# Inverting attention denominators four key steps later in the heads of two groups

## The reference

```python
def trunk_block(x, mods, g1, g2, w1, w2, mixer):
    sh1, sc1, gt1, sh2, sc2, gt2 = mods
    mixed, ctx_tensors = mixer(modulate(rmsnorm(x, g1), sh1, sc1))
    x = x + gt1 * mixed
    hh = modulate(rmsnorm(x, g2), sh2, sc2)
    x = x + gt2 * (jnp.square(jax.nn.relu(hh @ w1)) @ w2)
    return x, ctx_tensors
...
def swa_latent(q, k, v, kc, vc, sink):
    ...
    p = jax.nn.softmax(jnp.concatenate([s_loc, s_ctx, s_sink], axis=-1), axis=-1)
    ...
    out = (jnp.einsum('bnhgqk,bnkhd->bnqhgd', p_loc, vb)
           + jnp.einsum('bnhgqj,bjhd->bnqhgd', p_ctx, vc))
```

## Time and profile before

| | |
|---|---|
| median of 3 runs | 4050.73 us (4048.42 to 4055.04) |
| the profiled execution | 4054.53 us, of which its span is 4053.2 us |
| PE busy | 3846.6 us (95%) |
| DVE busy | 2080.5 us (51%) |
| ACT busy | 916.4 us (23%) |
| POOL busy | 576.0 us (14%) |
| mean granted clock of PE | 0.978 |
| attention of heads A0 to D3, layer 0 | from 681 us to 938 us |
| the same, layer 1 | from 2663 us to 2916 us |

### The profile page before, as it was taken

One profiled execution on the slowest core, in us unless ns is written; L12 is line 12 of the kernel. 1 busy time (PEld: TensorE's weight loads), 2 busy tenths in 40 slices (PEclk: granted clock), 3 DMA queues, 4 the chain that ended last, 5 costly groups with the idle time before them and its releaser, 6 DMA issues. The chain is left out here.

```text
span 4053.2 us, 47296 instructions
## 1 busy us (share of the span) xinstructions
PE 3846.6 (95%) x18444; PEld 2992.4 (74%) x18444; DVE 2080.5 (51%) x3428; ACT 916.4 (23%) x1718; POOL 576.0 (14%) x446
## 2 busy tenths in 40 slices
PE   6998999899999999999989989999999999999998
PEld 4787566565888888888868955666568888888886
DVE  5222555554465666665572245555546544455445
ACT  3111555443210000000031135544512000000002
POOL 0022011010211111111131111110021111111112
PEclk8999999999999999999999989999999999999999
DMA  6754224654022122112215433256340100110011
GB/s 235 228 180 127 64 55 95 136 133 167 32 73 73 37 73 73 63 47 73 64 52 184 138 98 79 51 125 146 89 167 32 42 32 32 42 42 32 32 42 52
DMA packets 289646, 358.53 MB, mean 88 GB/s; under 512 B 102994, under 2 KB 215508, under 8 KB 289296
## 3 DMA queue, kind: packets, MB, share of 16 engines
q1 hardware_dynamic: 269008, 350.54, 29.6%
q10 hardware_dynamic: 20416, 4.98, 0.6%
HBM read 288.28 MB, written 72.16 MB: 89 GB/s over the span
## 5 line engine op out<-in xcount | busy, mean ns | idle before, releaser
L2061 PE MATMUL bank<-h_hi,w_hi 128*128 128x512 f32 (+1 forms) x2496 | 906.1, 363 | 18.9 <-issue 14.5
L2062 PE MATMUL bank<-h_lo,w_hi 128*128 128x512 f32 (+1 forms) x2496 | 886.5, 355 | 0.0
L2063 PE MATMUL bank<-h_hi,w_lo 128*128 128x512 f32 (+1 forms) x2496 | 886.5, 355 | 0.0
L2218 PE MATMUL bank<-prob,vv 128*128 128x512 f32 (+3 forms) x1504 | 705.2, 551 | 0.0
L1879 DVE SCALAR_TENSOR_TENSOR xT<-bank,mods,xT 128x512 f32<-128x512 f32 (+1 forms) x816 | 536.5, 660 | 319.1 <-PE bank L2063 302.3
L2061 PE MATMUL bank<-m_hi,w_hi 128*128 128x512 f32 (+1 forms) x1536 | 569.9, 371 | 54.1 <-DVE xT L1879 51.8
L2061 PEld LDWEIGHTS bank<-h_hi,w_hi 128*128 128x128 f32 x2496 | 472.4, 189 | 100.8 <-issue 33.8
L2063 PE MATMUL bank<-m_hi,w_lo 128*128 128x512 f32 (+1 forms) x1536 | 546.7, 356 | 0.0
L2062 PE MATMUL bank<-m_lo,w_hi 128*128 128x512 f32 (+1 forms) x1536 | 545.5, 355 | 0.0
L1754 DVE TENSOR_REDUCE mp<-bank 128x1 f32<-128x512 f32 (+1 forms) x576 | 377.8, 659 | 295.3 <-PE bank L2164 294.4
L2062 PEld LDWEIGHTS bank<-h_lo,w_hi 128*128 128x128 f32 x2496 | 472.6, 189 | 73.2 <-issue 7.7
(11 more groups left out here) (188 smaller groups left out, 4025.8 us busy)
## 6 DMA issues: line engine op xcount, KB each, us to landing
stage<-in_w_mlp SPq DMA_DIRECT2D x64, 1024.0 KB, 5.2
nx_w<-in_w_ada SPq DMA_DIRECT2D x16, 1536.0 KB, 9.2
stage<-in_w_in SPq DMA_DIRECT2D x18, 1024.0 KB, 6.3
ada_h<-in_w_ada SPq DMA_DIRECT2D x16, 1024.0 KB, 7.8
rope_t<-in_k_rope SPq DMA_DIRECT2D x28, 512.0 KB, 4.9
k<-s_kB SPq DMA_DIRECT2D x48, 224.0 KB
k<-s_kA SPq DMA_DIRECT2D x24, 448.0 KB, 10.4
k<-s_kD SPq DMA_DIRECT2D x24, 448.0 KB, 10.5
```

Of the source, the lines that this page charges most:

```text
L2061: x = pe.matmul(out, a_hi, b_hi, start=first, stop=False)
L2062: pe.matmul(out, a_hi, b_lo, start=False, stop=False)
L2063: return x, pe.matmul(out, a_lo, b_hi, start=False, stop=last)
L2218: pe.matmul(ob[:, q0:q0 + n], vv[h % 2][:, key0 // P], prob[si % NP_RING][:, :n], start=(i == 0 and kind != "D"), stop=(i == len(steps) - ...
```

## The change

The inversions of RECIP_AT come four steps later, where the head in which they are done is of A or D; in the heads of B they stay.

```diff
-RECIP_AT = [STEP0[(v + 1) * NCH + 1] - 1 for v in range(NV - 1)]
+RECIP_AT = [STEP0[(v + 1) * NCH + 1] - 1 + (0 if JOBS[(v + 1) * NCH][0] == "B" else 4) for v in range(NV - 1)]
```

## The result

The changed kernel takes 4029.38 us (median of 5 runs, 4024.56 to 4035.81), the kernel before in the same comparison 4052.64 us. The ratio is 0.9943, with a 95% interval of 0.9932 to 0.9955: 23 us faster. 41 us were forecast, and a time from 3998 to 4026 us. The direction was right, the size was not.

A forecast was written before the change was run, and what follows sets the result against it. PE was taken as the bound, idling behind DVE's waits for denominators, worth 51.6 us. Less 0.5, 4.5, 0.6 and 5.0 this gave 41 us gained: 4010 us, range 3998 to 4026.

The forecast's parts named there:

- Bound and worth of the stalls: From A1's start to D3's, both layers: DVE's waits for denominators reach PE; the excess over unstalled heads is 51.6 us.
- The stall itself: DVE's wait at line 1798: arrival stays 20.4 us after A2's start; 58.2 us of waits fall to under 12.
- PE loses 0 to 0.3 us in each of A1, A2: In A1 and A2, both layers: some 1.0 us of DVE's wait is left, costing PE 0.5 us together.
- The Fourier loads behind the inversion: A0's Fourier loads delay A2's loads by 3.0 and 0.8 us, so A1's denominators come late: 4.5 us lost, bounds 0 and 8.
- The pair copies: In D0 and D2, ACT's output copy waits 2.0 us for POOL's product: 0.6 us on PE at once, 5.0 over SP.
- PE's own part: In D0 and D2, PE feels 0.3 us of ACT's 2.0 us wait, four times: 0.6 us after overlap.
- The part over SP: SP stores the pair before loading D2: PE waits 2.0 us more in D1 per layer, 5 us with slow clock.
- Sum: Whole kernel: 51.6 - 0.5 - 4.5 - 0.6 - 5.0 = 41 us gained, 4010 us as the median.
- The chances: Whole kernel: forecast (30 to 52 us gained) 0.77, another wait takes the place 0.14, no effect 0.05, slower 0.04.
- The first rival: Fourier issues, late pair and D1's load wait cost their upper bounds: 20 to 29 us gained, 4022 to 4031; chance 0.14.

The follow-up runs named there:

- the split load: The changed kernel with the Fourier load of 127 partitions made as two loads, of 112 and 15 partitions; 4014.30 us, ratio to before 0.9900.
- the kernel of 3998.70 us: The kernel with the split load and the steps by head, plus pair stored after next head's loads and query side of bias table first; ratio 0.9865.
- the kernel with the split load and the steps by head: Kernel before with the Fourier load split; inversions unmoved in A0, three steps later in D0 and D2, four in A1, A2, A3, D1, D3; 4009.21 us, ratio 0.9891.

## Why the prediction was wrong, point by point

**Bound and worth of the stalls: right, a little low.** 51.6 us were read from the heads' starts. With all waits over 0.4 us taken away, the same stretch gave 60.5 us. The 9 us more are in the two heads that served as measure: D2 with its 27.24 us had a gap of its own (0.73 us) and runs in 26.3 without it (D0 in 25.9), which makes 6.6 us over six D heads, and A0 with its 30.36 us is 0.3 to 0.5 us longer than A1 to A3 can be, 2.3 us over six A heads.

**The stall itself: right.** The denominators arrived where they had, 20.3 us after A2's start, and DVE's wait fell from 58.2 to 0.4 us. In A1 they came 3.8 to 4.0 us later than before, in both layers; the sum had 3.0 and 0.8. That this made no row of its own is no merit of the prediction: DVE was held up before it, by the table.

**"PE loses 0 to 0.3 us in each of A1, A2": wrong.** The step took it that behind the removed wait there was work ready to run. The first piece behind it had a wait of its own, for the bias table; the kernel before shows no row for it, since the table was in 15.9 us after A2's start and DVE came to it only at 20.4 us. It cost 1.3 us of PE in A2 and made the head 1.5 us too long. It could have been found in the code (line 1757 asks for the table) and in the time at which the table's loads land.

**The Fourier loads behind the inversion: mechanism named, size wrong.** 4.5 us were set for A1, with 8 us as the bound. Measured are 38.7 and 38.9 us instead of 30.0: 17.5 us, of which some 3 us are the table wait that A2 has too; leaving A0 alone gave back 14 us of it. Two steps of the sum failed. SP's lateness was 1.3 us, less than the 3.0 taken for layer 0, since one hold of 2.12 us (line 1043) was gone; in layer 1 it was 1.4 us, more than the 0.8 taken. And a landing was set equal to an issue: behind the load of 127 partitions a part of each load came late, and 1.3 us became 5 us. The wait that this lengthened was the table's; the prediction had it in the denominators. The 4.54 us that SP spent on the issue after that load was to be seen in the profile of before, and I didn't ask what it was.

**The pair copies: right in sum, not in its parts.** 5.6 us were set against the change; going from four to three steps gave back 5 us with the split load and about 6 us without. ACT waited 1.6 to 2.2 us for 2.0, SP's loads left 2.2 us later for 2.0. PE's own part was 1.2 to 1.6 us in each of four places, not 0.3 us: the values' two steps of lead hide only some 0.6 us. The part over SP was smaller than set: PE's wait for k in D1 grew from 1.26 to 1.50 us in layer 0 and from 1.55 to 2.81 in layer 1, 1.5 us together for 4. That the two errors cancel is luck.

**Sum.** Of the 60.5 us that the stretch can give, the changed kernel leaves 32.9: 17.5 in A1, 3.0 in A2, 10.7 in D1 and 1.6 in D2 (each head against its length in the kernel of 3998.70 us). That leaves 27.6 us, where the sum had 41. With three steps in D0 and D2 instead of four, the 12.3 us in D1 and D2 were 6.4, most of it around the wait for k that D1 had before the change. The profiled executions differ by 21.9: A0 of layer 0 started 3.1 us later already, before any changed place, and the rest lies elsewhere outside the stretch.

**The chances.** The first rival stood at 0.14, since its upper bounds (8 us in A1, 12 for the pairs) were taken as unlikely. The time of 4029 us lies in its range partly by luck: A1 went far beyond its bound, the pairs stayed at half of theirs, and the table was in none of its parts. The range ended at 4026 and so cut off most of it.

## What to carry to other kernels

A wait that is removed uncovers those behind it that had time to end in its shadow; they have no row in the profile, as the 18.4 us of waiting for the table had none before. So go through each semaphore that the next instructions ask for, and compare the time at which it is met with the new time of arrival.

Moving an instruction moves all that an in-order queue issues after it. Move only where the wait is (the one inversion here that had no stall to lose cost 14 us), as far as the arrival needs and no further: three steps for the heads with a copy close behind, four for the others.

Where an issue itself takes microseconds, find out which load stands in front of it before shifting it towards others.

## What the runs showed of the hardware that I had not expected

- A load of 127 partitions slowed loads issued behind it: the one-row load issued next held SP for 3.9 to 4.6 us instead of 0.25, and table loads took up to 14.5 us to land instead of 11. Two loads of 112 and 15 partitions did neither. Where the next head's loads left 11.3 us behind it instead of 7.7, the split made no difference in time (1.0006).
- A gap of 1.5 to 2 us in PE may or may not be followed by low clock: D0 in layer 0 of the kernel before was 29.62 us long and in layer 1 27.53 us, with gaps of 1.87 and 1.41 us. Nor does the longer gap decide: in the kernel with the split load and the steps by head, D1 had a gap of 1.77 us in layer 0 with a clock of 0.50 behind it (head 29.87 us), and one of 2.36 us in layer 1 with the full clock (28.85 us). What a stall costs is read from the head, not from the gap.
